# The last seventeen attention steps of a two-mixer decoder layer: order of work around one shared PSUM bank

## What is computed

```
q, k, v ..., z_a, q_g, k_g, v_g, a_low, z_b, merge = split(rms_norm(x) @ w_in)
log_a = log_sigmoid(a_low @ a_up + a_b) / 16
s = q @ k * scale - slope * dist;  p = masked_softmax(s);  o = p @ v        # three branches
b = cumsum(log_a);  q_dec = q_g * exp(b);  k_inv = k_g * exp(-b)           # GLA
S = exp(b_last) * S + k_tail @ v_g;  o_gla = q_dec @ S + tril(q_dec @ k_inv) @ v_g
y = x + (sigmoid(g_a) * (o_nsa @ w_ba) + sigmoid(g_b) * (o_g @ w_bb)) @ w_out
```

## Time and profile before

| | |
|---|---|
| median of 3 runs | 1310.61 us |
| the profiled execution | 1307.56 us |
| its span, first to last instruction | 1305.8 us |
| PE busy | 1271.5 us, 97% of the span |
| DVE busy | 678.7 us, 52% |
| ACT busy | 579.5 us, 44% |
| mean granted TensorE clock | 0.996 |

### The profile page before, as it was taken

The page is one execution under the profiler, slowest core; times in us unless marked ns, Lnnn a source line. Parts: engine busy times, 40 slices in busy tenths (PEclk is TensorE's granted clock), DMA queues, the critical chain, the costliest instruction groups (busy, mean ns, idle before and its releaser), DMA issues.

```text
span 1305.8 us, 23210 instructions
## 1 busy us (share of the span) xinstructions
PE 1271.5 (97%) x9281; PEld 1156.7 (89%) x9281; DVE 678.7 (52%) x1535; ACT 579.5 (44%) x1032; POOL 137.3 (11%) x181
## 2 busy tenths in 40 slices
PE   8999999999999999999999999999988999999998
PEld 6999999999989999999999999878866789999876
DVE  6212245655846556445454444667678666453332
ACT  6211336642446545355554545665377542221111
POOL 2100002103300000000002100202000392000000
PEclk9999999999999999999999999999999999999999
DMA  6341444522522222222122222655264856442231
GB/s 199 91 153 41 123 142 120 152 72 64 82 72 67 67 61 61 72 82 61 51 66 77 61 66 76 196 156 152 80 216 144 280 169 213 144 141 80 101 133 49
DMA packets 156764, 144.71 MB, mean 111 GB/s; under 512 B 27345, under 2 KB 141345, under 8 KB 156594
## 3 DMA queue, kind: packets, MB, share of 16 engines
q1 hardware_dynamic: 153872, 134.81, 34.0%
q0 software_dynamic: 2784, 8.43, 2.2%
q10 hardware_dynamic: 2, 0.00, 0.0%
HBM read 105.36 MB, written 41.88 MB: 113 GB/s over the span
## 4 chain that ended last, share of the span: by engine, by line
PE 68%; DVE 4%; ACT 2%; issue 1%; SPq 0%; DMA 0%; DVEq 0%; ACTq 0%
PE ps L250 39%; PE ps L2580 7%; PE ps L1695 5%; PE ps L1729 5%; PE ps L1711 4%; PE ps L2484 1%; PE ps L2452 1%; PE ps L2488 1%; PE ps L1801 1%; DVE sP L2053 1%; PE ps L2588 1%; PE ps L1644 1%; PE ps L1661 1%; PE ps L2543 1%; DVE S L2692 0%
## 5 line engine op out<-in xcount | busy, mean ns | idle before, releaser
L250 PE MATMUL ps<-hH,wH 128*128 128x352 f32 (+1 forms) x1288 | 426.9, 331 | 2.1 <-DVE hL L599 1.1
L250 PE MATMUL ps<-hH,wL 128*128 128x352 f32 (+1 forms) x1288 | 414.5, 322 | 0.0
L250 PE MATMUL ps<-hL,wH 128*128 128x352 f32 (+1 forms) x1288 | 413.4, 321 | 0.0
L250 PEld LDWEIGHTS ps<-hH,wH 128*128 128x128 f32 (+1 forms) x1288 | 240.7, 187 | 23.6 <-issue 19.7
L250 PEld LDWEIGHTS ps<-hL,wH 128*128 128x128 f32 (+1 forms) x1288 | 242.0, 188 | 2.2 <-issue 1.9
L250 PEld LDWEIGHTS ps<-hH,wL 128*128 128x128 f32 (+1 forms) x1288 | 240.9, 187 | 0.3
L228 DVE TENSOR_TENSOR wL<-w_raw,wH 128x1024 fp32r<-128x1024 f32 (+1 forms) x70 | 86.1, 1231 | 155.7 <-ACT wH L220 155.5
L387 ACT ACTIVATE stg<-ps 128x352 f32<-128x352 f32 x132 | 61.1, 464 | 228.6 <-PE ps L250 223.1
L220 ACT ACTIVATE wH<-w_raw 128x1024 fp32r<-128x1024 f32 (+1 forms) x70 | 73.3, 1048 | 66.6 <-issue 39.5
L2287 ACT ACTIVATE sP<-sP,stat 128x640 f32<-128x640 f32 (+7 forms) x128 | 92.7, 727 | 0.3
L2031 DVE CUSTOM_DVE_ANT_0 sP<-ps,dist,stat 128x256 f32<-128x256 f32 (+3 forms) x116 | 57.9, 541 | 38.0 <-PE ps L1695 31.4
(11 more groups left out here) (394 smaller groups left out, 2018.9 us busy)
## 6 DMA issues: line engine op xcount, KB each, us to landing
w_raw<-in_w_in SPq DMA_DIRECT2D x61, 512.0 KB, 3.9
p_spill<-stg SPq DMA_DIRECT2D x132, 176.0 KB, 1.9
zt<-p_spill SPq DMA_DIRECT2D x24, 528.0 KB, 4.9
w_raw<-in_w_in SPq DMA_DIRECT2D x17, 256.0 KB, 4.1
gvT<-p_spill SPq DMA_DIRECT2D x8, 528.0 KB, 5.8
x_all<-in_x_prompt SPq DMA_DIRECT2D x8, 512.0 KB, 8.2
m_raw<-in_w_branch_b SPq DMA_DIRECT2D x8, 512.0 KB, 5.4
xr<-in_x_prompt SPq DMA_DIRECT2D x8, 512.0 KB, 3.5
```

The costliest lines, as they stand in the source:

```text
L250: mm = nc.tensor.matmul(ps[0:t.m, bank, 0:NF], w[:, c % 2, t.m * k:t.m * k + t.m], x[n][:, k, :], start=(k == 0 and i == 0), stop=(k == t. ...
```

## The change

Seven edits, all in the tail and the head after it.

PE's tail loop:

```
-                slot(t, 0)
+                if m < ncut - 1:
+                    slot(t, 0)
                 transposes(m)
+                if m == ncut - 1:
+                    slot(t, 0)
+                early = ncut - 1 > m >= ncut - LA
+                if early:
+                    slot(t, 1)
                 values(m - 1)
-                slot(t, 1)
+                if not early:
+                    slot(t, 1)
```

DVE's tail step and its pieces of the GLA heads:

```
                 t = m - M0
+                if t == 4:
+                    slot(t, 0)
                 scales(m + 2)
-                slot(t, 0)
+                if t not in (4, 16):
+                    slot(t, 0)
                 copies(m)
+                if t == 16:
+                    slot(t, 0)
                 slot(t, 1)
+                slot_part(t)
                 if m + LA < ncut:
                     score(m + LA)
                 slot(t, 2)
```

In step 4 `copy_probs(0)` comes ahead of the scaling; in step 16 `copy_probs(5)` comes behind `copies(65)`. `slot_part(t)` is new. It takes from `head_part`, which stands at the step's end, these pieces, and puts them between places 1 and 2:

```
+            def slot_part(t):
+                if t == 14:
                     dve.wait_ge(sem("u_done"), NU)
                     for n in (2, 3, 4):
                         dve.wait_ge(sem(f"p_stored{n}"), 16 * ((NU - n + NSTG - 1) // NSTG))
                     later_queries(link, 0)
                     dve.wait_ge(sem("qk_done"), ncut)
                     inputs(0)
                 elif t == 16:
                     log_sigmoid(dve, link, 1)
```

More of the change, by code:

```diff
@@ L2163, in head_part, with slot_part @@
                 elif t == 14:
+                    minus_abs(dve, 1)
+                elif t == 15:
+                    tail_sums(link, 0)
+                    link(nc.vector.tensor_reduce(bmt4[:, :, :], own, AX, ALU.add))
+                    link(nc.vector.tensor_reduce(bmt[:, :], bmt4[:, :, :], AX, ALU.add))
+            def slot_part(t):
+                if t == 14:
                     dve.wait_ge(sem("u_done"), NU)
-                    minus_abs(dve, 1)
                     for n in (2, 3, 4):
@@ L2170, in head_part @@
                     inputs(0)
[L2171 to L2174, removed]
                 elif t == 16:
                     log_sigmoid(dve, link, 1)
-                    minus_abs(dve, 2)
             rows = 0
@@ L2717, in first_head @@
                 masked(0, 1)
+                minus_abs(dve, 2)
                 state(0, 0)
```

## The result

The changed kernel takes 1300.76 us (median of 4 runs, 1299.05 to 1301.14); beside it the kernel before took 1310.15 (4 runs, 1306.87 to 1310.77). The ratio is 0.9931, with the interval 0.9912 to 0.995. The forecast was faster, by 5.4 us, at 1305.2, with 1303.0 to 1308.0 as its range. The profiled execution took 1299.05 us, its span 1297.0, at a mean granted clock of 0.997; before it was 1307.56, 1305.8 and 0.996. The question of this study is therefore why it came out 8.5 us faster by the profiled executions and 9.4 by the medians, and not 5.4.

The account below looks back on a forecast made before the run. PE, busy 97% of the span, was taken to bound the kernel, so only its waits and lower-clock stretches could pay. Terms 2.6 + 0.7 + 1.9 = 5.2, plus 0.2 for hand-overs, gave 1310.61 - 5.4 = 1305.2 us, range 1303.0 to 1308.0.

Parts of the forecast that it names:

- Step 4: PE's 2.27 us wait ahead of rest 0 goes, about 1.0 appears ahead of values 0, full clock returns: 2.6 us gained.
- Step 13: PE's 0.69 us wait ahead of probs 4 for ACT's copy of page 14 is hidden by values(61): 0.7 us gained.
- the 0.2 that the sum held for hand-overs: Across the edits, 0.2 us gained from shorter hand-overs where two users are parted.
- Step 14: PE gains nothing, the 0.89 us wait of scores 5 stays; on DVE z_score(5) starts 1.0 us late.
- Steps 15, 16 and the first head: Tail's end into head 0: PE waits fall, some new ones appear, ACT sets head 0's pace: 1.9 us gained.
- the sum's last line: Whole kernel: runs' median lies 3.05 us above the profiled execution, so 1310.61 - 5.4 = 1305.2 us.
- The clock still falls in step 4: Rival: PE's clock still falls in or behind step 4; gain 4.0 us, 1306.6 us; chance 0.14.
- The clock better: Rival: the stretches in step 4 and at 1030 to 1034 both stay at full clock; 1.5 us more, 1303.7; chance 0.10.
- The tail gives nothing: Rival: late z_score(5) delays ACT's chain, or head 0 takes DVE's pace; gain 3.3 us, 1307.3 us; chance 0.12.
- Slower: Rival: short waits in steps 14 to 16 and head 0 drop PE to 1.2 GHz; 1312.7 us; chance 0.04.

Follow-up runs that it names:

- before_b: The kernel before, unchanged, in a single execution for another profile: 1309.72 us.
- before_c: The kernel before, unchanged, in a single execution for another profile: 1306.72 us.
- no_early: The changed kernel with place 1 behind the values again on PE in steps 13 to 15, DVE as changed: 1302.02 us in a single execution.
- after_again: The changed kernel, unchanged, in five rounds beside the kernel before: 1301.54 us, ratio 0.9945.
- before_d: The kernel before, unchanged, in a single execution for another profile: 1306.39 us.
- step4_only: The kernel before with only the step 4 edit, copy_probs(0) ahead of the scaling on DVE: 1304.16 us, ratio 0.997.
- tail_only: The changed kernel with the step 4 edit undone and all else kept: 1300.88 us, ratio 0.9954.
- rest_first: The changed kernel with copies(53) and copy_rest(0) also ahead of the scaling in step 4 on DVE: 1298.81 us, ratio 0.9942.
- tuned: rest_first with, on DVE, z_score(5) ahead of the scaled queries in step 14 and tail_sums(0) behind copy_rest(5) in step 16: 1299.22 us, ratio 0.9947.
- abs_back: The changed kernel with minus_abs(2) back at the end of step 16, ahead of drain(7): 1302.71 us in a single execution.

## Why the prediction was right in direction and wrong in time

**Step 4 (2.6; 2.7 measured).** The interval fell from 21.05 to 18.35. The split was also right: 1.26 for the order (1.3) and 1.44 for the clock (1.4). But the second only counts in executions where the stretch was there: three of before's four profiles, not the fourth. What a stretch costs can be read in three places: 1.50 us for the one in step 4, 3.41 us long, with the little that lies behind the interval; 2.78 for those of before_b and before_c, 6.83 us long; and 1.05 for the one in head 2, again 3.41 us long (below). That is 0.44, 0.41 and 0.31 us for each microsecond at half clock. The Trainium skill ("TensorE: Matmul & The Clock Gate", Terms) would price these stretches at length times one minus the granted share, that is 1.7, 3.4 and 1.7 us. The measurement decides: the rule is an upper bound here. Waits of PE within a stretch, such as the 0.65 us at 951 in before_c, account for a part in the tail; in head 2 PE is busy throughout the stretch, and why it costs least there stays open.

**Step 13 (0.7; 0.97 measured).** The wait of 0.69 is gone. The rest is the other hand-over, as no_early gives back 0.95 with the same edit: part of the 0.2 that the sum held for hand-overs.

**Step 14 (nothing; 0.00 measured).** 3.73 before and after. `z_score(5)` was late by what the products take, and their own wait cost nothing.

**Steps 15, 16 and the first head (1.9; 2.12 measured).** The waits went or came as worked out, the largest error being 0.15 us; only one of 0.15 ahead of `rest 5` was not forecast. That the gain lasts, because ACT sets head 0's pace, holds: 1.26 ahead of the core product in both kernels.

**The order of the work alone** is thus worth 1.26 + 0.97 + 2.12 = 4.35 us, against 5.4 - 1.4 = 4.0 in the sum. The mechanisms of the order were right and their sizes within 0.35 us together. The lowest execution of each kernel says much the same without any price for the clock: 1302.26 us among 49 of before, 1298.22 among ten of after, 4.0 apart.

**The step that failed is the sum's last line,** "The median of the runs lies 3.05 us above the profiled one, so I forecast 1310.61 - 5.4", together with the clock, which had one term of 1.4 there. Two things were wrong with it.
- *The base.* Over the 45 executions of before that came later its mean is 1307.33 us and its median 1306.98; with the four of the first comparison the mean is 1307.50 over 49. Three executions at 1310 were the upper part of a spread from 1302.3 to 1312. The 3.05 us were no fixed distance but another draw from it. The forecast lay 1305.2 - 1300.8 = 4.4 us too high, and 1310.61 - 1307.50 = 3.1 of that is the base. The 9.4 us of the first comparison hold some 3 us of it too: with more executions the difference is 6.7 to 7.2 (after_again's rounds) or 6.5 to 6.7 (means: 1307.33 or 1307.50, against 1300.85 over 10).
- *The clock outside step 4.* The mean granted clock is 0.9958 over the 45 executions of before and 0.9978 over the ten of after. What is missing to 1 is half the time at half clock: 2 x (1 - 0.9958) x 1306 = 11.0 us before and 2 x (1 - 0.9978) x 1299 = 5.7 after, 5.3 us less in an execution. At the 0.31 to 0.44 us just measured for each microsecond, that is an estimated 1.6 to 2.3 us. With the order's 4.35 it is 6.0 to 6.7, and 6.5 to 7.2 were measured; the start (below), which can differ by 2.1 us between two executions, is not in this sum. The prediction had 1.4 for the clock, since it took the granted clock as the one trace had it, with stretches at fixed places. before_b and before_c show that before has them in other places in other executions, and before_d that the one in head 2 can be missing.

The difference of the first two profiles, 8.8 us of span, can be laid out: 2.70 in step 4, 0.97 in step 13, 2.12 in tail and head, 1.72 at the start (below), and 1.05 in GLA head 2, where the stretch at 1030 is missing from this trace of after. That is 8.56; the rest, 0.2, is not placed. The last term is read on PE from its wait of 0.83 us for `ATs` to the next one, of 0.34 us for `kt`. In before it is 1036.61 - 1027.46 = 9.15:

```profile
1027.46 0.62 PE L2514 MATMUL ps<-S,qd 128*4 128x256 f32 x8 [0.83 <-DVE ATs L2686]
...
1036.61 1.53 PE L2452 MATMUL ps<-vh,kt 128*128 128x256 f32 x6 [0.34 <-ACT kt L1546]
```

and in after 1027.93 - 1019.83 = 8.10:

```profile
1019.83 0.61 PE L2530 MATMUL ps<-S,qd 128*4 128x256 f32 x8 [0.83 <-DVE ATs L2702]
...
1027.93 1.53 PE L2468 MATMUL ps<-vh,kt 128*128 128x256 f32 x6 [0.34 <-ACT kt L1546]
```

**What the clock does, and what is only argued.** With less waiting on PE the mean granted clock rises over the executions of six kernels:

```
kernel       executions   mean us    mean granted clock
before       45           1307.33    0.9958
step4_only   6            1304.12    0.9968
tail_only    6            1301.81    0.9973
after        10           1300.85    0.9978
rest_first   6            1298.87    0.9980
tuned        6            1299.23    0.9985
```

The steps between the rows are small beside the spread within one kernel, whose executions have mean clocks from 0.992 to 0.999 before and from 0.997 to 0.999 after. before_b and before_c have their 6.8 us stretches where three of the waits of the earlier trace rows, 0.70, 1.08 and 0.65 us, follow within 4 us, the last of them inside the stretch. Of five profiles with the tail's old order two have such a stretch, of seven with the new order none. But after_again and abs_back have one of 3.4 us a little later, at 979 in head 0, and rest_first one at 1041. That fewer waits are the cause is therefore argued and not shown: so few profiles don't exclude chance, and no run moved the waits about without changing their sum. What also stays open is why the clock falls within a microsecond of the end of the wait of 2.27 us in step 4 in three profiles and not in before_c or tail_only, and why the same waits and the same busy share in the tail bring the fall in two profiles and not in before, before_d and step4_only.

**The rivals.** *The clock still falls in step 4*: no profile with the copies ahead has it. *The clock better* (1303.7) was the nearest one, right in kind, but priced for one stretch of one trace, and at 1.5 us where the traces show 1.05. *The tail gives nothing* fell with the 2.12. *Slower*, half clock in steps 14 to 16, was set down for the changed kernel; the traces show the mechanism in the kernel before, twice in four profiles. The Trainium skill ("TensorE: Matmul & The Clock Gate", section "A second HAM failure mode: psum-queue depth-cycling") has such a rule, and I set it aside because one trace of before did not have it; before_b and before_c agree with it, with 6.8 us at half clock in a part full of short waits, and before, before_d and step4_only, with the same waits, don't show it. If the rule holds here, it speaks for this change and not against it.

## What to carry to other kernels

Read a gain between two marks of the same engine, where the intervals here repeated to 0.05 us, and forecast the whole time from the mean of many executions: three runs of a kernel whose own spread is 9.6 us say little of its level. Ask of a stretch at a lower clock in which share of the executions it is there, and treat the clock as a term of the whole kernel: removing waits was worth 4.35 us by the order, and some 2 more came with a better clock, though that the waits were its cause is not shown. And a wait removed is worth its length less what then comes up behind it: 0.55 of 0.80 in abs_back, 0.29 of 0.96 in tuned.

## What the runs showed of the hardware that was not expected

**The first 40 us vary by 2.1 us,** in a part that no edit touches. The first matmul of the input projection's unit, in the profile before:

```profile
40.16 0.43 PE L250 MATMUL ps<-hH,wH 128*128 128x352 f32 x1 [1.07 <-DVE hL L599]
```

and in the profile after:

```profile
38.44 0.43 PE L250 MATMUL ps<-hH,wH 128*128 128x352 f32 x1 [1.07 <-DVE hL L599]
```

It starts between 38.4 and 40.6 over the profiles. It goes with when PE comes to the full clock. The same eight transposes (line 442) begin at 12.0 to 12.9 us in every trace. They take 1.06 or 1.07 us in the six that start the projection by 39.6, and also in before_b, which starts it at 40.4 and has 6.8 us at half clock from 14.2 on. They take 1.94 us in the other five, which start it at 40.0 to 40.6; there the next eight, at 21.1 to 21.7, take 1.03 or 1.04. Even an early full clock is lost again for a while, as the profile after has it from 10 to 20, with 0.83:

```profile
10.00:20.00 10.00, 7.64 (x43) 7.21 (x42) 9.38 (x13) 8.64 (x15) 1.49 (x2) 0.83 1.02 313
```

**Stretches at half clock** were, in all profiles and but for the last 1 to 4 us of each, 3.4 or 6.8 us long, and one kernel had them in different places from one execution to the next: 859 and 1030 in before; 14, 861 and 953 in before_b; 14, 949 and 1007 in before_c; 859 in before_d. The kernel after had one at 14, and in after_again one at 979; no_early had none from 21 us to its last 4 us.
